# Two transformer blocks on one core: the first input groups without their norm, the last output chunk by pairs, FFN inputs two steps ahead, no filler products at the boundaries

## What is computed

```
# first block, 2 layers; norm(v) = v / sqrt(mean(v*v) + eps)
for layer in (0, 1):
    if layer == 1: build shared k, v from norm(x)*scale + shift          # kv, with a compression MLP
    for sub in (0, 1, 2):
        h = norm(x) * g_pre * (1 + scale) + shift
        y = swiglu_ffn(h)            if sub in (0, 2)                     # 1024 -> 2 x 2816 -> 1024
        y = short_conv_mixer(h)      if sub == 1 and layer == 0
        y = nsa_attention(h, k, v)   if sub == 1 and layer == 1
        x = x + w * gate * g_post * norm(y)
# second block, 2 layers
for layer in (0, 1):
    h = norm(x) * g * (1 + scale) + shift
    q, k, v, g, u, s, p, gates = split(h @ w_in)                          # 1024 -> 24 groups of 512 columns ...
    x = x + gate * (merge(retention, spatial_gating, pooling) @ w_out)
    h = norm(x) * g * (1 + scale) + shift
    x = x + gate * (relu(h @ w_ff1) ** 2 @ w_ff2)                         # 1024 -> 4096 -> 1024
return norm(x) * final_norm
```

## Time and profile before

| | |
|---|---|
| median of three runs | 2322.74 us |
| the profiled execution | 2319.62 us |
| its span | 2317.9 us |
| TensorE busy | 2239.9 us, 97% |
| VectorE busy | 1521.0 us, 66% |
| ScalarE busy | 972.3 us, 42% |
| GpSimd busy | 165.4 us, 7% |
| mean matmul clock | 0.975 of full |
| read from HBM | 491.73 MB, 213 GB/s over the span |

### The profile page before, as it was taken

The page is one execution under the profiler, slowest core; times in us unless marked ns, Lnnn a source line. Parts: engine busy times, 40 slices in busy tenths (PEclk is TensorE's granted clock), DMA queues, the critical chain, the costliest instruction groups (busy, mean ns, idle before and its releaser), DMA issues.

```text
span 2317.9 us, 42296 instructions
## 1 busy us (share of the span) xinstructions
PE 2239.9 (97%) x18080; PEld 2203.8 (95%) x18080; DVE 1521.0 (66%) x1720; ACT 972.3 (42%) x941; POOL 165.4 (7%) x285
## 2 busy tenths in 40 slices
PE   6999999999999998899999999999999999999998
PEld 6999999999999997699999999999999999999997
DVE  6876568877457874778866345768875445666554
ACT  3433444334333344553344444344444444335442
POOL 0110001110001100211100000001100000000000
PEclk8999999999779997999999999999999999999999
DMA  9996457995459942069964545548985545444552
GB/s 339 353 337 237 144 183 273 332 325 181 128 206 338 329 155 91 1 212 338 337 224 155 163 128 176 171 164 304 368 283 161 182 128 170 158 168 160 182 181 73
DMA packets 264591, 494.67 MB, mean 213 GB/s; under 512 B 17040, under 2 KB 146448, under 8 KB 264208
## 3 DMA queue, kind: packets, MB, share of 16 engines
q1 hardware_dynamic: 229760, 366.47, 47.1%
q0 software_dynamic: 34704, 126.37, 14.5%
HBM read 491.73 MB, written 1.05 MB: 213 GB/s over the span
## 4 chain that ended last, share of the span: by engine, by line
PE 93%; DVE 4%; ACT 1%; DMA 1%; issue 1%; SPq 0%; DVEq 0%; ACTq 0%
PE PA L469 15%; PE PA L471 15%; PE PA L470 15%; PE PY L469 7%; PE PY L471 7%; PE PY L470 7%; PE PB L469 5%; PE PB L470 5%; PE PB L471 5%; PE PA L519 2%; PE PB L512 2%; DVE wlo L1262 1%; DVE rstd L1304 1%; DMA mix<-adat 1%; PE PY L917 1%
## 5 line engine op out<-in xcount | busy, mean ns | idle before, releaser
L1262 DVE TENSOR_TENSOR wlo<-raw,whi 128x2048 fp32r<-128x2048 f32 x335 | 764.7, 2286 | 439.9 <-ACT whi L943 333.1
L469 PE MATMUL PA<-opA_hi,whi 128*128 128x256 f32 x2528 | 718.5, 284 | 1.8 <-DVE opA_lo L1315 1.8
L471 PE MATMUL PA<-opA_hi,wlo 128*128 128x256 f32 x2528 | 717.2, 284 | 0.0
L470 PE MATMUL PA<-opA_lo,whi 128*128 128x256 f32 x2528 | 717.2, 284 | 0.0
L943 ACT ACTIVATE whi<-raw 128x2048 fp32r<-128x2048 f32 x203 | 384.9, 1902 | 283.3 <-PE PA L471 140.3
L469 PEld LDWEIGHTS PA<-opA_hi,whi 128*128 128x128 f32 x2528 | 487.3, 193 | 2.5 <-issue 2.5
L470 PEld LDWEIGHTS PA<-opA_lo,whi 128*128 128x128 f32 x2528 | 487.3, 193 | 0.1
L471 PEld LDWEIGHTS PA<-opA_hi,wlo 128*128 128x128 f32 x2528 | 487.1, 193 | 0.0
L469 PE MATMUL PY<-opB_hi,whi 128*128 128x256 f32 x1344 | 381.2, 284 | 9.8 <-DVE opB_lo L1373 6.0
L470 PE MATMUL PY<-opB_lo,whi 128*128 128x256 f32 x1344 | 380.3, 283 | 0.0
L471 PE MATMUL PY<-opB_hi,wlo 128*128 128x256 f32 x1344 | 380.3, 283 | 0.0
(11 more groups left out here) (245 smaller groups left out, 2761.5 us busy)
## 6 DMA issues: line engine op xcount, KB each, us to landing
raw<-ffn_w_in SPq DMA_DIRECT2D x176, 512.0 KB, 5.2
mix<-adat POOLq DMA_DIRECT2D x144, 512.0 KB, 6.4
raw<-w_in SPq DMA_DIRECT2D x144, 512.0 KB, 4.7
raw<-w_ff SPq DMA_DIRECT2D x128, 512.0 KB, 4.5
adaw<-adat POOLq DMA_DIRECT2D x96, 512.0 KB, 6.5
raw<-ffn_w_out SPq DMA_DIRECT2D x88, 512.0 KB, 4.5
raw<-w_branch SPq DMA_DIRECT2D x48, 512.0 KB, 4.6
raw<-a_w_in SPq DMA_DIRECT2D x24, 512.0 KB, 4.6
```

The costliest lines, as they stand in the source:

```text
L469: nc.tensor.matmul(o_, w1, rhs(xh), start=start, stop=False, skip_group_check=True)
L470: nc.tensor.matmul(o_, w1, rhs(xl), start=False, stop=False, skip_group_check=True)
L471: return nc.tensor.matmul(o_, w2_, rhs(xh), start=False, stop=stop, skip_group_check=True)
L1262: TT(wlo[slot][:, 0:w], raw[slot][:, 0:w], whi[slot][:, 0:w].bitcast(F32), ALU.subtract).then_inc(lo_ready, 1)
```

## The change

Five things are changed together.

1. **The first input groups take x without its norm.** At each of the nine boundaries between stages the operand is z = x * scale, and two columns are added to the 256 (`ZC` = 258): the shift's high and low part. The products of the first two groups of 512 columns (three in kv; four single chunks in `ff2`) run on it, one bank for each 128 columns: group one in PA and PB, group two in PY. The statistics of x are summed by GpSimd (`acc_x`), and two small products (`xnorm`) bring them to all partitions: in TensorE's order they stand in the first chunk of group two, after two row blocks. VectorE evacuates each bank as result * rstd into `zt` and sums the two extra columns into `zb` (`zevac`), and ScalarE adds that bias while it copies on (`zcopy`, or in silu and relu). The normed operand is made meanwhile (`pre`) and written over z, for the third group onwards.
2. **y's norm.** Row blocks 0 to 5 of the squares are summed by VectorE (accy), so that only three statistics products are left, one of them early. VectorE interleaves u, the add and the low part of z; all adds of x are VectorE's.
3. **The last output chunk by pairs.** It goes through its columns in pairs of 128 (`out_rows` with a tag), so that the banks of PY are finished one after the other. The output is written in four DMAs.
4. **FFN inputs two steps ahead** (`FFN_SEQ`: in 0, in 1, in 2, out 0, in 3, out 1, ...; `FF2_SEQ` five ahead); hidden parts use two or four places of operand B. The loops are written out.
5. **The ring** has four slots, and `wlo` lies on the same addresses as `raw`. So a slot is loaded when its chunk is multiplied, and no longer when its low part is made. **No filler** is left at the boundaries.

```
-RING = 3
+RING = 4
-GAP_Y, GAP_X, GAP_B = 22, 16, 5
+GAP_Y = 0
+ZC = T + 2
+FFN_SEQ = [("in", 0), ("in", 1), ("in", 2)] + [x_ for j in range(FFN_STEPS - 3) for x_ in (("out", j), ("in", j + 3))] + \
+    [("out", j) for j in range(FFN_STEPS - 3, FFN_STEPS)]
+FF2_SEQ = [("in", j) for j in range(5)] + [x_ for j in range(FF2_STEPS - 5) for x_ in (("out", j), ("in", j + 5))] + \
+    [("out", j) for j in range(FF2_STEPS - 5, FF2_STEPS)]
...
-        raw = [sb(f"raw{i}", [P, CHUNK]) for i in range(RING)]
-        wlo = [sb(f"wlo{i}", [P, CHUNK], F32R) for i in range(RING)]
+        ring_at = [SBUF_TOP - 4 * CHUNK * (i + 1) for i in range(RING)]
+        raw = [nc.alloc_sbuf_tensor_at(f"raw{i}", [P, CHUNK], F32, offset=ring_at[i]) for i in range(RING)]
+        wlo = [nc.alloc_sbuf_tensor_at(f"wlo{i}", [P, CHUNK], F32R, offset=ring_at[i]) for i in range(RING)]
...
# SyncE
-                    sp.wait_ge(lo_ready, c - (RING - 1))
+                    sp.wait_ge(multiplied, c - (RING - 1))
...
# TensorE
+            def zchunk(c, banks, tile, kts, sub, hook=None, half=False):
+                pe.wait_ge(lo_ready, c + 1)
+                slot = c % RING
+                for kk, k in enumerate(kts):
+                    need(pe, "V", f"{sub}.zlo{k}")
+                    if hook and kk == 2:
+                        hook()
+                    for m, o_ in enumerate(banks):
+                        w_ = slice(tile(kk, m), tile(kk, m) + P)
+                        nc.tensor.matmul(o_[:, 0:ZC], whi[slot][:, w_], wide[:, k, :], start=k == 0, ...)
+                        nc.tensor.matmul(o_[:, 0:T], whi[slot][:, w_], opl["A"][:, k, :], ...)
+                        last = nc.tensor.matmul(o_[:, 0:ZC], wlo[slot][:, w_], wide[:, k, :], ...)
...
             def boundary(sub, nsub):
                 take("A")
                 if not sub.startswith("b"):
-                    ssq_pairs(f"{sub}.y")
+                    take("B")
+                    need(pe, "V", f"{sub}.acc")
+                    nc.tensor.matmul(PB[:, 0, :], onesD, accy[:], start=True, stop=False)
+                    need(pe, "S", f"{sub}.ysq3")
+                    nc.tensor.matmul(PB[:, 0, :], onesD, tmp8[:, 6, :], start=False, stop=False)
+                    S(nc.tensor.matmul(PB[:, 0, :], onesD, tmp8[:, 7, :], start=False, stop=True), f"{sub}.yssq")
                     idle(GAP_Y)
-                    ssq(f"{nsub}.x", 1)
-                else:
-                    idle(GAP_B)
-                    ssq(f"{nsub}.x")
-                if nsub != "fin":
-                    idle(GAP_X)
...
+            zpair(CH["conv_in"], "01", ("conv0", "conv1"))
+            for g in range(2, 6):
...
# ScalarE
             def boundary(sub, nsub, c_done, c_next):
+                load_table(ACT.Sqrt)
                 prep_to(c_next + 2)
...
+                prep_to(c_next + 3)
+                for k in range(KT):
+                    need(act, "V", f"{sub}.x{k}")
+                    if nsub != "fin":
+                        if not first:
+                            act.wait_ge(multiplied, c_done - (1 if k < 6 else 0))
+                        S(AC(oph["A"][:, k, :], x[:, k, :], ACT.Copy, scale=A_(nsub)[:, k:k + 1]), f"{nsub}.zhi{k}")
+                    S(AC(tmp8[:, k, :], x[:, k, :], ACT.Square), f"{nsub}.sq{k}")
+            def zcopy(name, dst, scale=None):
+                need(act, "V", f"{name}.z")
+                for m in range(4):
+                    S(AC(dst[m], zt[:, m, :], ACT.Identity, bias=zb[:, m:m + 1]), name)
...
# VectorE
+            def zevac(name, bufs, rows=P, scale=None):
+                for i, n_ in enumerate(bufs):
+                    n = 4 if n_ == "Y" else 2
+                    ps = flat[n_].rearrange("p (m e) -> p m e", e=512)
+                    v = S(TT(zt[:, 2 * i:2 * i + n, :], ps[:, :, 0:T], rstd[:].unsqueeze(1).broadcast_to([P, n, T]), ALU.mult))
+                    v = S(nc.vector.tensor_reduce(zb[:, 2 * i:2 * i + n], ps[:, :, T:ZC], AX.X, ALU.add), f"{name}.z")
...
+            c = CH["conv_in"]
+            prep_to(c + 5)
+            inverse("01")
+            prep_to(c + 6)
+            zevac("conv0", "AB")
+            pre("01", tmp8, c + 7)
+            need(dve, "S", "conv0")
+            dve.wait_ge(multiplied, c + 4)
+            zevac("conv1", "Y")
...
# GpSimd
-            def add_x(sub):
-                for k in POOL_ADDS:
-                    need(pool, "V", f"{sub}.u{k}")
-                    S(pool.tensor_tensor(x[:, k, :], x[:, k, :], tmp8[:, k, :], ALU.add), f"{sub}.x{k}")
+            def acc_x(nsub):
+                for k in range(1, KT):
+                    need(pool, "S", f"{nsub}.sq{k}")
+                    S(pool.tensor_tensor(accx[:], tmp8[:, 0, :] if k == 1 else accx[:], tmp8[:, k, :], ALU.add), f"{nsub}.acc")
```

More of the change, by code:

```diff
@@ L743, in _ @@
             by("Y", "V", "scmp")
+            take("A")
+            need(pe, "S", "gate")
+            for ic in range(2):
+                last = nc.tensor.transpose(flat["A"][:, ic * 48:ic * 48 + 48], gfm[0:48, ic * P:ic * P + P], ident[0:48, 0:48])
+            S(last, "gt")
+            by("A", "S", "gexp")
             scores(1)
@@ L1243, in _ @@
                 else:
[L1244 to L1245 removed]
+                    boundary("b11", "fin", N_CHUNKS, N_CHUNKS)
         @block.vector
```

871 lines of the change are left out of this document (490 added, 381 removed).

## The result

The changed kernel is slower: 2346.36 us (median of 4 runs, 2344.23 to 2350.71) against 2323.04 us (4 runs, 2322.64 to 2323.85), ratio 1.0102 with a 95% interval of 1.0085 to 1.0120. The forecast was 2291 us, range 2254 to 2320. The profiled execution, the fastest of the four, spans 2342.3 us where the one before spans 2317.9: 24.4 us more.

A forecast was written before the change was run, and what follows sets the result against it. TensorE, busy 97% of the span, was taken as the bound. Gains of 88.8 us less 12 (clock), 44.4 (new waits) and 1 gave 31.4 off the profiled 2319.62; with 3.1 to the median, 2291 us, range 2254 to 2320.

The forecast's parts named there:

- Gaps of the first block: Six first-block boundaries, 95.6 us in all: each gap was to shrink to 6.3 us, saving 57.8 us.
- accy and the first three squares lie beside the last chunk: First-block boundaries: this part of y's statistics was to run during the last chunk's products, within the 6.3 us gap estimate.
- Gaps of the second block: Three second-block boundaries: each gap was to be 3.0 us instead of 8.8, saving 17.4 us.
- The end: Tail of the kernel after the last products: 11.0 us instead of 14.6, saving 3.6 us.
- Inputs two steps ahead: Last output chunks of four FFNs and two second FFNs: all six waits of 1.67 us go, saving 10.0 us.
- What is late next: New waits, mainly before third groups, also kv, attention, first mix, second FFNs: 44.4 us lost; bounds 0 and twice that.
- The load term: Third-group wait chain: the load of chunk 5 into its freed slot was taken to last 5.6 us.
- The clock: Six first-block gaps without filler: a fall to half clock at each, 2.0 us apiece, 12 us lost.
- rival 2: Half clock takes the filler's place at all nine gaps, plus falls at third-group waits: 2313 us, chance 0.13.
- the bound of 24: Upper bound on the clock loss: falls at all nine boundaries, each costing the full 2.7 us.
- Pitch: Products with two extra columns, 32 of 48 in each of 36 chunks: 1 us lost.
- rivals 2 and 3: The second of these: the ring starves TensorE in five stages with modulation work, 2352 us at 1 us per step, chance 0.10.

The follow-up runs named there:

- a2_accfirst: Changed kernel with squares of y and accy ahead of the next stage's second-chunk cast and low part; third chunk's cast moved mid-loop at second-block boundaries: 2336.3 us.
- a4_onestep: Changed kernel with the FFN inputs one step ahead, as before the change, instead of two: 2366.7 us.
- c1_slabs: Changed kernel with the first five modulation slabs of FFNs 2 and 3 issued ahead of GpSimd's adds of x squared, likewise for kv: 2332.4 us.
- a3_normfirst: Changed kernel with the norm one weight chunk earlier in the queues of ScalarE and VectorE in all nine stages: 2328.3 us.
- b4_hifirst: Kernel before with the ring's high parts placed ahead of the raw weights in SBUF, only these two changing place: 2322.6 us.
- b2_place: Kernel before with only its buffers moved: high parts first, low parts last and offset by 32 bytes: 2306.4 us.
- b3_place0: Kernel before with only its buffers moved, high parts first, low parts last at a multiple of 64 bytes: 2289.1 us.
- a9_align: Changed kernel with the low parts and the rows of the widened operand at multiples of 64 bytes: 2338.4 us.
- b1_nofill: Kernel before with no filler products at its nine boundaries and nothing else changed: 2346.6 us.

## Why the prediction was wrong

- **Gaps of the first block (57.8 forecast, 30.4 measured).** The links of the chain were right, its pace a little too fast: from the first statistics product on it takes 6.0 to 7.4 us (6.8 from 235.38 to 242.15, 7.4 from 555.22 to 562.60), where the same links sum to 5.4 in the forecast. Most of the difference is the statistics: three products take 1.5 to 2.9 us, the longer ones in part at half clock, instead of two in 0.87. The step that failed is "accy and the first three squares lie beside the last chunk". They are in the order behind a cast whose load lands late, and behind reductions. What the runs showed in its place: two gaps kept their 16 us, with TensorE waiting up to 9.12 us for accy, and those two alone are 20 us of the miss; a2_accfirst, which moves one cast and one low part behind the squares, gives 10 us back. The comparison of the orders showed a cast ahead of the first high part on ScalarE, which I priced for the second block; I did not price what stood ahead of the squares.
- **Gaps of the second block (17.4, 14.5 measured).** Right in mechanism; two are 2.8 us, the third is 6.8 us, because there the third chunk's cast waits for its transfer until 1779.48, 3.9 us after the last product.
- **The end (3.6, 0.9 measured).** Still 3.00 us of waiting for accx behind it; mis-sized.
- **Inputs two steps ahead (10.0).** Right: no idle of 1.5 us stands before any last output chunk. a4_onestep shows that the changed kernel needs them for more than that.
- **What is late next (44.4, 74 measured: 64.0 plus the 10.0 that went).** The mechanism was right, place and kind: third group, released by the normed low part, kv, second FFNs. The size was not. The load term was 5.6 us and measured 8.6 to 10.2 in FFN 2, because modulation slabs share the DMA engines (c1_slabs has 3.5 to 5.7), and the second FFNs wait 16.8 and 10.6 us in all where I had 6.7 each (3.1 and 3.6). In the first of them a low part whose cast waits 11.9 us for a transfer stands ahead of the reciprocal (a3_normfirst took 5 us off it, and nothing off the second). The largest of their waits, 7.6 and 5.5 us, stand before output 0, behind the evacuation of PY, a kind that I had priced only in FFNs 2 and 4. That part 5 of the change puts a transfer ahead of every cast is in the forecast's count for chunk 5, but not as a debit of all stages; what the ring alone costs stays open, since no run gave the changed kernel its three slots or a `wlo` of its own back. My upper bound of twice 44.4 held it, but I had let it into the range by half only.
- **The clock (12, 30.4 measured).** The six first-block gaps cost what was forecast: the slow products right behind them take 12.5 us too long. Those behind the three second-block gaps add 4.0, and the rest, about 15 us, stands behind the waits of the third groups and of output 0, as rival 2 said. That is above the bound of 24 that I gave, because the bound counted nine gaps and not the waits behind them. Rival 2's own reasoning (24 plus 10) came nearest. TensorE is at half clock for 151 us more than before. The Trainium skill ("TensorE: Matmul & The Clock Gate", section "HAM oscillation — how this bites in real kernels") takes half of the throttled time as lost, which as an estimate would be 75 us. The trace does not agree: it shows 30 us, since the slow products fill only some 70 of the 151 us (334 more of them, 0.21 us each) and the rest passed in waits, statistics and the attention.
- **Pitch (1, -25.1 measured).** 22.2 us of it are the pitch proper. No row of before hinted at it and no term of the forecast stood for it: the change moved the ring to other addresses. This gain is luck.

The time lies between rivals 2 and 3 and is neither: the mechanisms are the forecast's and rival 2's, with gains too large and debits too small, and on top a gain of 22 us from the pitch that no case had. The range varied the debits alone, by half, and took the gains as certain; the gains came out 33 us short, and both erred in part for one cause, the weight chunks at a stage's start.

## What to carry to other kernels

Where in-order queues serve both a stage's end and the next one's start, read what stands ahead of each link of the new chain, and take transfer times from rows with the same traffic, not from a median over the kernel. Price filler like any product: 21 products at a boundary gave 7 us here, 34 or 50 cost 5. Compare versions at equal buffer placement: here the order of allocations alone was worth 33 us, more than the 23 that the change cost.

## What the runs showed of the hardware

- Product pitch depends on where the buffers lie: 0.1200 (before, b4_hifirst), 0.1190 (b2_place), 0.1185 (changed) or 0.1178 us (b3_place0, a9_align) for the same 128x128 by 256 product at full clock.
- The Trainium skill ("TensorE: Matmul & The Clock Gate", section "Back-to-back issue gap") gives N/2.4 + 2.5 ns for one isolated product behind another, as an estimate 109 ns for 256 columns, and says that in a stream with weight loads the spacing is set by both. The traces here lie above that estimate, at 117.8 to 120.0 ns.
- A filler of 128x128 in fp32 takes 0.228 us at full clock, in two records; two statistics products of 256 columns take 0.87 us at full clock and 2.05 at half (b1_nofill).
- The 512 KB halves of a chunk land in 3.5 to 5.7 us where no slabs stand ahead of them (c1_slabs), in 8.6 and 10.2 us right behind five slabs, and in 8.7 and 11.5 us beside slabs and the attention's constants, at 391 to 392 GB/s.
